# A two-layer hybrid block with PEER experts: the PEER stage unrolled, v gathered by token and summed in column tiles, with rings of four buffers

## The chip, the cores and the metric

One core of one Trainium2 chip runs the whole program. The metric is the device time of one execution in microseconds. PE is TensorE, DVE VectorE, ACT ScalarE, POOL GpSimd, SP SyncE.

## What is computed

Two layers over 512 latent and 256 context tokens of width 1024, in float32. Each layer is a mixer (convolution, retention, mLSTM, windowed attention, a gated merge, an output projection) and then PEER, a feed-forward part made of experts, on which the change falls. Layer 0 applies PEER to all 768 tokens (6 blocks of 128), layer 1 to the 512 latent tokens (4 blocks).

```python
def block(xb):                                   # 128 tokens
    q = (xb @ wq).reshape(-1, HEADS, 2, half)
    s = jnp.einsum('nhcd,ckd->nhck', q, keys)    # 8 heads, 2 sides, 128 keys
    sv, si = lax.top_k(s, 16)
    cand = sv[:, :, 0, :, None] + sv[:, :, 1, None, :]
    cv, ci = lax.top_k(cand.reshape(..., 256), 16)
    expert = i1 * 128 + i2                       # i1, i2 picked from si by ci
    gate = jax.nn.softmax(cv, axis=-1)
    u_sel, v_sel = u[expert], v[expert]          # (n, 8, 16, 1024) each
    act = gelu(einsum('nd,nhkd->nhk', xb, u_sel))
    return einsum('nhk,nhkd->nd', gate * act, v_sel)
```

Each token thus needs 128 rows of `u` and 128 rows of `v`, its 128 slots (head h, rank k, n = 16 h + k), and each row is 4 KB. A block gathers 2 x 128 x 128 rows.

## The kernel before

All engines run through stages in the same order; at a stage's start each waits for all to have ended the one before. The stages of a layer are norm, ret, mlstm, attn, merge, out, peerq, route, peer. Every result of PE outside the PEER sum goes through a rotation of PSUM banks: `bank(name)` takes the next one and first waits until the bank taken `BANKS` names earlier has been read (`BANKS` is 8).

The stage peer is a loop (`eng.Fori`) on each engine over the blocks of `peer_calls(l)`: one loop over the 2 context blocks and one over the 4 latent blocks in layer 0, one over 4 in layer 1. In a block:

- POOL issues one indirect DMA per slot. `u` of slot n brings to partition p the row of token p (L2000), into a ring of 8 buffers of 128 x 1024. `v` of slot n does the same (L2008) into another ring of 8, and follows 16 slots behind `u`: 16 `u` alone, then 112 times `u` and `v` in turn, then 16 `v` alone. `u` waits for the dot that frees its buffer, `v` for the PE sum that frees its own. POOL issues in program order, so what waits holds up all behind it.
- DVE takes the dot product of each landed `u` with the block's activations (L1566). Between the dots it does the routing of the next block in pieces (`route_part`): `top_keys` and `candidates` in heads 0 to 3, one of them after every fourth dot; `pick_keys` twice in head 4 (it ends at L1481); small ones after. It does so in the last block of a layer too, whose result nobody reads. After each head `weigh` multiplies gates and activations.
- ACT takes the gelu of a head's 16 dots and then makes 16 diagonal 128 x 128 matrices of weights (L1891), in a ring of 8.
- PE multiplies each diagonal with its `v` (L854, L856) and accumulates all 128 slots in banks 6 and 7: tokens are rows there.
- At the block's end DVE waits for the last sum, scales it in PSUM (L1577), and adds it to the residual (L1581, L1586). The next block begins with copies (L1526 to L1533) and its first dot.

## Time and profile before

| what | value |
|---|---|
| median of 3 runs | 7287.52 us (7281.2 to 7294.59) |
| the profiled execution | 7279.13 us, its span 7277.3 us |
| PE, DVE, ACT, POOL busy | 5493.0, 3590.4, 967.0, 2810.0 us |
| moved | 1580.75 MB, of it 1363.67 MB by POOL's queue |
| gathers | 1280 of `u`, 1280 of `v` |

The span runs from the first to the last instruction; some microseconds of an execution lie around it. Busy time is a mean over stages with different limits, so the stage is read by itself: POOL is busy only in PEER, from 2055 to about 4309 us and from 5758 to about 7260 us, and there the DMA engines are busy nearly all the time.

### The profile page before, as it was taken

What the parts mean: (1) busy time and instruction counts of PE and PEld (TensorE: products, weight loads), DVE (VectorE), ACT (ScalarE), POOL (GpSimd) and SP (SyncE); (2) the same over time, 40 slices, a digit from 0 to 9 for tenths busy, and PEclk for the clock granted to TensorE, in tenths of its full rate; (3) what the DMA queues carried; (4) which work ended last, traced back from release to release, by engine and by line L of the source; (5) the groups of instructions that cost most, each with busy time, mean ns of one, the idle gap of its engine ahead of it and who ended that gap; (6) DMA issues with size and microseconds to landing.
All of it is one profiled execution on the core that took longest, in us unless ns stands there. A gap on an engine that the chain in (4) does not pass through costs nothing. (4 is left out here: it accounts for less than half of the span.)

```text
span 7277.3 us, 56488 instructions
## 1 busy us (share of the span) xinstructions
PE 5493.0 (75%) x16472; PEld 2983.1 (41%) x16472; DVE 3590.4 (49%) x7999; ACT 967.0 (13%) x2360; POOL 2810.0 (39%) x2627
## 2 busy tenths in 40 slices
PE   3869699999966666656666668788999765766666
PEld 1545657556632222222222235465646422222222
DVE  1565645112455555656565635455312664646474
ACT  1102012000011111111111120111200111111111
POOL 0000000000057677767676740000000276767676
PEclk7979785999988888889888889888699888888888
DMA  8101100111279999999999971021023599999998
GB/s 331 41 12 41 64 24 1 67 52 64 93 256 375 337 368 353 371 343 370 348 369 335 370 277 47 29 73 32 13 92 103 183 368 344 369 353 372 341 363 343
DMA packets 556363, 1580.75 MB, mean 217 GB/s; under 512 B 73665, under 2 KB 207297, under 8 KB 555953
## 3 DMA queue, kind: packets, MB, share of 16 engines
q0 software_dynamic: 374032, 1363.67, 49.7%
q1 hardware_dynamic: 182048, 213.91, 8.9%
q8 instruction: 105, 1.72, 0.1%
q14 instruction: 178, 1.45, 0.1%
HBM read 1572.95 MB, written 4.44 MB: 217 GB/s over the span
## 5 line engine op out<-in xcount | busy, mean ns | idle before, releaser
L854 PE MATMUL bank<-arena 128*128 128x512 f32 x2560 | 1443.7, 647 | 1292.0 <-ACT arena L1891 1028.8
L2000 POOL DMA_INDIRECT arena<-in_peer_u,arena x1280 | 1354.0, 1058 | 2509.4 <-issue 2383.1
L1566 DVE CUSTOM_DVE_ANT_0 arena<-arena 128x1024 f32<-128x1024 f32 x1280 | 1551.3, 1225 | 1174.8 <-DMA arena<-in_peer_u,arena 1149.3
L2008 POOL DMA_INDIRECT arena<-in_peer_v,arena x1280 | 1421.6, 1111 | 420.5 <-issue 294.8
L856 PE MATMUL bank<-arena 128*128 128x512 f32 x2560 | 1371.3, 619 | 0.0
L854 PEld LDWEIGHTS bank<-arena 128*128 128x128 f32 x2560 | 482.0, 203 | 2090.6 <-ACT arena L1891 1095.9
L516 PE MATMUL bank<-arena 128*128 128x512 f32 (+3 forms) x2880 | 935.3, 488 | 4.8 <-DVE arena L949 3.2
L856 PEld LDWEIGHTS bank<-arena 128*128 128x128 f32 x2560 | 513.5, 201 | 665.4 <-issue 665.4
L516 PEld LDWEIGHTS bank<-arena 128*128 128x128 f32 x2880 | 533.5, 193 | 400.2 <-issue 338.7
L1891 ACT ACTIVATE arena<-arena 128x128 f32<-128x128 f32 x1280 | 453.3, 395 | 1600.4 <-PE bank L856 894.1
L781 PE MATMUL bank<-arena 128*128 128x512 f32 (+1 forms) x1536 | 569.2, 524 | 1.7 <-ACT arena L1805 1.7
L781 PEld LDWEIGHTS bank<-arena 128*128 128x128 f32 x1536 | 294.2, 192 | 260.5 <-issue 244.6
L1927 POOL DMA_DIRECT2D arena<-in_mlstm_gate_b x8 | 4.1, 522 | 811.4 <-DVE arena L1080 811.4
L1356 DVE TENSOR_TENSOR arena<-bank,arena 128x256 f32<-128x256 f32 (+1 forms) x72 | 43.4, 603 | 535.2 <-PE bank L786 535.2
L786 PE MATMUL bank<-arena 128*128 128x512 f32 (+1 forms) x768 | 290.7, 522 | 0.0
L1882 ACT ACTIVATE arena<-arena 128x16 f32<-128x16 f32 x80 | 17.4, 217 | 1616.2 <-DVE arena L1566 1616.2
L527 PE MATMUL bank<-arena 128*128 128x256 f32 (+1 forms) x960 | 193.9, 365 | 28.6 <-DVE arena L895 28.6
L989 DVE SCALAR_TENSOR_TENSOR arena<-arena 128x512 f32<-128x512 f32 (+1 forms) x360 | 207.0, 658 | 0.0
L786 PEld LDWEIGHTS bank<-arena 128*128 128x128 f32 x768 | 146.2, 190 | 128.7 <-issue 122.3
L527 PEld LDWEIGHTS bank<-arena 128*128 128x128 f32 x960 | 171.7, 195 | 53.4 <-issue 32.7
L1927 POOL DMA_DIRECT2D arena<-mlstm_rows x24 | 12.8, 536 | 403.8 <-DVE arena L1249 133.9
L1577 DVE TENSOR_TENSOR bank<-bank,arena 128x512 f32<-128x512 f32 x20 | 13.0, 694 | 292.5 <-PE bank L856 292.5
(270 smaller groups left out, 4628.0 us busy)
## 6 DMA issues: line engine op xcount, KB each, us to landing
arena<-in_w_in SPq DMA_DIRECT2D x74, 1024.0 KB, 5.3
arena<-in_mod_w SPq DMA_DIRECT2D x24, 2048.0 KB, 18.1
arena<-in_peer_wq SPq DMA_DIRECT2D x32, 1024.0 KB, 5.6
arena<-in_peer_u,arena POOLq DMA_INDIRECT x1280, 6.2
arena<-in_peer_v,arena POOLq DMA_INDIRECT x1280, 6.3
arena<-mlstm_rows POOLq DMA_DIRECT2D x24, 768.0 KB, 4.4
arena<-in_w_branch SPq DMA_DIRECT2D x32, 512.0 KB, 6.3
arena<-mod_rows SPq DMA_DIRECT2D x16, 512.0 KB, 8.0
```

The source lines that it names most:

```text
L516: i = mm(b[:, 0:n], w[:, k, m * P:(m + 1) * P], HTk[:, k, t0:t0 + n], start=(k == 0), stop=(k == KD - 1))
L527: i = mm(b[:, 0:n], HTk[:, k, t * P:(t + 1) * P], w[:, k, c0:c0 + n], start=(k == 0), stop=(k == KD - 1))
L781: i = mm(b[:, 0:n], wg[:, k, m * P:(m + 1) * P], HTk[:, k, t0:t0 + n], start=(k == 0), stop=(k == KD - 1))
L786: i = mm(b[:, 0:n], wb[:, k, m * P:(m + 1) * P], YSb[:, i_ * BB + k, t0:t0 + n], start=(k == 0), stop=(k == BB - 1))
L854: mm(banks[6][:, :], G["diag"][:, n % DRING, :], G["v"][n % VRING][:, 0:512], start=(n == 0), stop=(n == SLOTS - 1))
L856: mm(banks[7][:, :], G["diag"][:, n % DRING, :], G["v"][n % VRING][:, 512:1024], start=(n == 0), stop=(n == SLOTS - 1)).then_inc(fl.sem("v ...
L989: v.scalar_tensor_tensor(dst, src, tap, dst, ALU.mult, ALU.add).then_inc(*dv.step())
L1356: v.tensor_tensor(PRD[:, 0:n], b[:, 0:n], g, ALU.mult).then_inc(*dv.step("read", ("branch", l, j, i_, m, t0)))
L1566: v.tensor_tensor_reduce(u, u, G["hb"], 1.0, 0.0, ALU.mult, ALU.add, G["dots"][:, n:n + 1])\
L1891: act(G["diag"][:, n % DRING, :], ident, ACT.Copy, scale=G["w"][:, n:n + 1])\
L2000: eng.indirect_dma_start(G["u"][n % URING], None, utab, bass.IndirectOffsetOnAxis(G["idxu"][:, n:n + 1], 0))\
L2008: eng.indirect_dma_start(G["v"][n % VRING], None, vtab, bass.IndirectOffsetOnAxis(G["idxv"][:, n:n + 1], 0))\
```

## The change

- The loops go: each engine's program is written out for all blocks, waits are for constants, and the copies at a block's start go (buffers alternate by block instead). `route_part` is left out in a layer's last block.
- `v` is gathered by token: gather n brings to partition p the row of slot p of token n. For this the indices are transposed on PE (`turned`, `turned_indices`), and so are the weights; ACT's `spread` writes them into two zeroed tensors so that `token_weights(G, n)` is a 128 x 32 matrix with one filled column. The diagonals go.
- PE sums token n with four matmuls of 128 x 32 by 128 x 256, one in each column tile (`tile_position=(0, 32 * j)`). A row of PSUM is then a token within its group of 32, and a tile holds 256 of its columns; after the scaling, SP turns the result back to tokens by columns with 16 small DMAs a block (`yp` to `yt`), and DVE adds it later.
- A layer with B blocks has B + 1 passes. In pass x POOL issues `u` of block x and `v` of block x - 1 in turn: the first pass is `u` alone, the last `v` alone.
- The rings of `u` and `v` have 4 buffers each, and the rotation of banks has 6, since banks 6 and 7 are kept for the sums.

```diff
-BANKS = 8
-URING, VRING, DRING = 8, 8, 8
+BANKS = 6
+URING, VRING = 4, 4
+IDX_RING = 3
...
+def peer_blocks(l):
+    first = 0 if l == 0 else NB + (l - 1) * (NB - CB)
+    return [(first + x, t) for x, t in enumerate(out_blocks(l))]
...
+            ws = [HT[:, 2 * D:2 * D + 64 * 32], ws1]
+                        idxu=[iu.bitcast(U32)[:, x * SLOTS:(x + 1) * SLOTS] for x in range(2)],
+                        idxt=[it.bitcast(U32)[:, x * SLOTS:(x + 1) * SLOTS] for x in range(IDX_RING)],
+                        gate=[gt[:, x * SLOTS:(x + 1) * SLOTS] for x in range(2)],
+                        u=ring[:URING], v=ring[URING:URING + VRING],
...
+        def token_weights(G, n):
+            g, m = divmod(n, 32)
+            return G["ws"][g // 2][:, g % 2, 32 * m:32 * m + 32]
...
-                for b0, nb, base in peer_calls(l):
-                    with eng.Fori(0, nb) as i:
-                        for n in range(SLOTS):
-                            if n == 0:
-                                eng.wait_ge(fl.sem("residual_added"), i + base + 1)
-                            eng.wait_ge(fl.sem(f"v_landed{n % VRING}"), (i + base) * (16 * SLOTS // VRING) + 16 * (n // VRING + 1))
-                            eng.wait_ge(fl.sem("diagonal_ready"), (i + base) * SLOTS + n + 1)
-                            mm(banks[6][:, :], G["diag"][:, n % DRING, :], G["v"][n % VRING][:, 0:512],
-                               start=(n == 0), stop=(n == SLOTS - 1))
-                            mm(banks[7][:, :], G["diag"][:, n % DRING, :], G["v"][n % VRING][:, 512:1024],
-                               start=(n == 0), stop=(n == SLOTS - 1)).then_inc(fl.sem("v_summed"), 1)
+                def turned(name, src, ready):
+                    b = bank(name)
+                    eng.wait_ge(*at(*ready))
+                    nc.tensor.transpose(b[:, 0:P], src, ident).then_inc(*pe.step("full", name))
+                def v_sum(it, n):
+                    g, m = divmod(n, 32)
+                    if n == 0:
+                        eng.wait_ge(*at("spread", it))
+                        if it > peer_blocks(l)[0][0]:
+                            eng.wait_ge(*at("y_scaled", it - 1))
+                    eng.wait_ge(*at("v_landed", it, n))
+                    for j in range(COLS):
+                        i = mm(banks[6 + g // 2][32 * j:32 * j + 32, (g % 2) * W:(g % 2 + 1) * W], token_weights(G, n),
+                               G["v"][(it * SLOTS + n) % VRING][:, j * W:(j + 1) * W], start=(m == 0), stop=(m == 31),
+                               tile_position=(0, 32 * j))
+                    i.then_inc(*pe.step("v_summed", it, n))
+                blocks = [it for it, _ in peer_blocks(l)]
+                turned(("idxT", blocks[0]), G["i2"], ("experts", blocks[0]))
+                for it in blocks + [blocks[-1] + 1]:
+                    for n in range(SLOTS):
+                        if it > blocks[0]:
+                            v_sum(it - 1, n)
+                        if n == (HEADS - 1) * TOPK and it + 1 in blocks:
+                            turned(("idxT", it + 1), G["i2"], ("experts", it + 1))
+                    if it in blocks:
+                        turned(("wT", it), G["w"], ("weighed", it, HEADS - 1))
...
+                def turned_indices(r, it):
+                    eng.wait_ge(*at("full", ("idxT", it)))
+                    v.tensor_copy(G["idxt"][it % IDX_RING], bank_of(("idxT", it))[:, 0:P]).then_inc(*r.step("idxt", it))
+                    fl.mark(("read", ("idxT", it)), r.sem)
...
+                for a in G["ws"]:
+                    v.memset(a, 0.0).then_inc(*dv.step("spread_zero", l))
+                turned_indices(dv, first)
...
+                def scaled_sum(it, t):
+                    s = 0 if t >= CB else 1
+                    if it > first:
+                        eng.wait_ge(*at("y_turned", it - 1))
+                    eng.wait_ge(*at("v_summed", it, SLOTS - 1))
+                    for half in range(2):
+                        v.tensor_tensor(G["yp"][:, half * 512:half * 512 + 512].rearrange("p (g c) -> p g c", g=2),
+                                        banks[6 + half][:, :].rearrange("p (g c) -> p g c", g=2),
+                                        G["ga"][:, s * W:(s + 1) * W].unsqueeze(1).to_broadcast([P, 2, W]), ALU.mult)\
+                            .then_inc(*dv.step("y_scaled", it))
+                def added_sum(it, t):
+                    eng.wait_ge(*at("y_turned", it))
+                    v.tensor_tensor(Xb[:, t, :], Xb[:, t, :], G["yt"], ALU.add).then_inc(*dv.step("x_done", it))
...
+                blocks = peer_blocks(l)
+                for x, (it, t) in enumerate(blocks):
+                    for h in range(HEADS):
+                        for k in range(TOPK):
+                            n = h * TOPK + k
+                            u = G["u"][(it * SLOTS + n) % URING]
+                            eng.wait_ge(*at("u_landed", it, n))
+                            v.tensor_tensor_reduce(u, u, G["H2"][:, t * D:(t + 1) * D], 1.0, 0.0, ALU.mult, ALU.add,
+                                                   G["dots"][:, n:n + 1]).then_inc(*dv.step("dot", it, n))
+                            if h and k == 3:
+                                weigh(it, h - 1)
+                            if it + 1 <= blocks[-1][0]:
+                                route_part(it + 1, STORE[:, x * NSCORE:(x + 1) * NSCORE], h, k)
+                            if x and h == 1 and k == 0 and x > 1:
+                                added_sum(it - 2, t - 2)
+                    weigh(it, HEADS - 1)
+                    if x:
+                        scaled_sum(it - 1, t - 1)
+                scaled_sum(it, t)
+                added_sum(it - 1, t - 1)
+                added_sum(it, t)
...
+                def spread(it):
+                    eng.wait_ge(*at("spread_zero", l))
+                    if it > peer_blocks(l)[0][0]:
+                        eng.wait_ge(*at("v_summed", it - 1, SLOTS - 1))
+                    eng.wait_ge(*at("full", ("wT", it)))
+                    b = bank_of(("wT", it))
+                    for half in range(2):
+                        act(G["ws"][half][:, :, 0:1024:33], b[:, half * 64:half * 64 + 64].rearrange("p (g m) -> p g m", g=2),
+                            ACT.Copy).then_inc(*sc.step("spread", it))
+                    fl.mark(("read", ("wT", it)), sc.sem)
+                for it, _ in peer_blocks(l):
+                    for h in range(HEADS):
+                        gelu(it, h)
+                        if h == HEADS - 3 and it + 1 <= peer_blocks(l)[-1][0]:
+                            gate_exp(it + 1)
+                    spread(it)
...
+                def u_gather(it, n):
+                    x = it * SLOTS + n
+                    if n == 0:
+                        eng.wait_ge(*at("idxu", it))
                         eng.sem_inc(fl.sem("gathers_allowed"), 1)
-                        for h in range(HEADS + 1):
-                            if h == 1:
-                                eng.wait_ge(fl.sem("v_indices_staged"), it + 1)
-                                eng.wait_ge(fl.sem("v_summed"), it * SLOTS + 1)
-                                eng.sem_inc(fl.sem("gathers_allowed"), 1)
-                            for k in range(TOPK):
-                                n = h * TOPK + k
-                                if h < HEADS:
-                                    if n >= URING:
-                                        eng.wait_ge(fl.sem("dots_done"), it * SLOTS + n - URING + 2)
-                                        eng.sem_inc(fl.sem("gathers_allowed"), 1)
-                                    eng.indirect_dma_start(G["u"][n % URING], None, utab,
-                                                           bass.IndirectOffsetOnAxis(G["idxu"][:, n:n + 1], 0))\
-                                        .then_inc(fl.sem(f"u_landed{n % URING}"), 16)
-                                if h:
-                                    n -= TOPK
-                                    if n >= VRING:
-                                        eng.wait_ge(fl.sem("v_summed"), it * SLOTS + n - VRING + 2)
-                                        eng.sem_inc(fl.sem("gathers_allowed"), 1)
-                                    eng.indirect_dma_start(G["v"][n % VRING], None, vtab,
-                                                           bass.IndirectOffsetOnAxis(G["idxv"][:, n:n + 1], 0))\
-                                        .then_inc(fl.sem(f"v_landed{n % VRING}"), 16)
+                    if x - URING >= peer_blocks(l)[0][0] * SLOTS:
+                        eng.wait_ge(*at("dot", *divmod(x - URING, SLOTS)))
+                        eng.sem_inc(fl.sem("gathers_allowed"), 1)
+                    fl.done(eng.indirect_dma_start(G["u"][x % URING], None, utab,
+                                                   bass.IndirectOffsetOnAxis(G["idxu"][it % 2][:, n:n + 1], 0)),
+                            f"u_landed{x % URING}", ("u_landed", it, n), by=16)
+                def v_gather(it, n):
+                    x = it * SLOTS + n
+                    if n == 0:
+                        eng.wait_ge(*at("idxt", it))
+                        eng.sem_inc(fl.sem("gathers_allowed"), 1)
+                    if x - VRING >= peer_blocks(l)[0][0] * SLOTS:
+                        eng.wait_ge(*at("v_summed", *divmod(x - VRING, SLOTS)))
+                        eng.sem_inc(fl.sem("gathers_allowed"), 1)
+                    fl.done(eng.indirect_dma_start(G["v"][x % VRING], None, vtab,
+                                                   bass.IndirectOffsetOnAxis(G["idxt"][it % IDX_RING][:, n:n + 1], 0)),
+                            f"v_landed{x % VRING}", ("v_landed", it, n), by=16)
+                blocks = [it for it, _ in peer_blocks(l)]
+                for it in blocks + [blocks[-1] + 1]:
+                    for n in range(SLOTS):
+                        if it in blocks:
+                            u_gather(it, n)
+                        if it > blocks[0]:
+                            v_gather(it - 1, n)
...
-                        dma(G["ga"][:, s * D:(s + 1) * D], modr[l, s:s + 1, 5 * D:6 * D].to_broadcast([P, D]), "ga2_loaded")
+                        for j in range(COLS):
+                            dma(G["ga"][32 * j:32 * j + 32, s * W:(s + 1) * W],
+                                modr[l, s:s + 1, 5 * D + j * W:5 * D + (j + 1) * W].to_broadcast([32, W]), "ga2_loaded")
                     fl.mark(("ga2", l), "ga2_loaded")
                     if l + 1 < DEPTH:
                         layer_vectors(l + 1)
+                    for it, t in peer_blocks(l):
+                        eng.wait_ge(*at("y_scaled", it))
+                        if it > peer_blocks(l)[0][0]:
+                            eng.wait_ge(*at("x_done", it - 1))
+                        for g in range(4):
+                            for j in range(COLS):
+                                dma(G["yt"][32 * g:32 * g + 32, j * W:(j + 1) * W],
+                                    G["yp"][32 * j:32 * j + 32, g * W:(g + 1) * W], "y_turned")
+                        fl.mark(("y_turned", it), "y_turned")
```

What stands on POOL at the start of layer 0's stage, before (the first two gathers wait for `dots_done` of the block before and then of the ring; the register instructions work out what to wait for):

```order
L2000 DMA arena<-in_peer_u,arena 128x1024 [waits dots_done]
L2000 DMA arena<-in_peer_u,arena 128x1024 x7
L1998 REGISTER_ALU
L2000 DMA arena<-in_peer_u,arena 128x1024 [waits dots_done]
L1998 REGISTER_ALU
L2000 DMA arena<-in_peer_u,arena 128x1024 [waits dots_done]
L1998 REGISTER_ALU
L2000 DMA arena<-in_peer_u,arena 128x1024 [waits dots_done]
```

After, from the ring's second round in the first pass to the first `v` (`peer0_vector` counts DVE's steps of the stage, the dots among them):

```order
L1993 DMA arena<-in_peer_u,arena 128x1024 x3
L1993 DMA arena<-in_peer_u,arena 128x1024 [waits peer0_vector] x125
L2006 DMA arena<-in_peer_v,arena 128x1024 [waits peer0_vector]
L1993 DMA arena<-in_peer_u,arena 128x1024 [waits peer0_vector]
L2006 DMA arena<-in_peer_v,arena 128x1024
L1993 DMA arena<-in_peer_u,arena 128x1024 [waits peer0_vector]
L2006 DMA arena<-in_peer_v,arena 128x1024
```

The first pass holds 128 `u` and no `v` (three and 125 of them stand here, after the first one), and what bounds its pace is a wait for the dot four slots back; before, `v` joined after 16 `u` and the wait was for the dot eight back.

What stands on DVE from the last dots of a block to the next, before (ISA is the dot and the reading of its sum):

```order
L1566 ISA arena<-arena 128x1024 [waits u_landed7]
L1566 ISA arena 128x1
L1572 COPY arena<-arena 128x128
L1541 REGISTER_ALU
L1542 TENSOR_TENSOR arena<-arena 128x16 [waits gelu_done]
L1575 ISA
L1577 TENSOR_TENSOR bank<-bank,arena 128x512 [waits v_summed]
L1577 TENSOR_TENSOR bank<-bank,arena 128x512
L1581 ISA [waits y_scaled]
L1581 TENSOR_TENSOR arena<-arena,bank 128x512
L1586 ISA [waits half_added,indices_staged]
L1586 TENSOR_TENSOR arena<-arena,bank 128x512
```

After, from the last dot of layer 0's second block on:

```order
L1580 ISA arena<-arena 128x1024 [waits u_landed3]
L1580 ISA arena 128x1
L1536 TENSOR_TENSOR arena<-arena 128x16 [waits peer0_scalar]
L1562 TENSOR_TENSOR arena<-bank,arena 128x512 [waits peer0_tensor]
L1562 TENSOR_TENSOR arena<-bank,arena 128x512
L1580 ISA arena<-arena 128x1024 [waits u_landed0]
L1580 ISA arena 128x1
L1580 ISA arena<-arena 128x1024 [waits u_landed1]
L1580 ISA arena 128x1
L1580 ISA arena<-arena 128x1024 [waits u_landed2]
L1580 ISA arena 128x1
```

The wait for `v_summed` stood for this block's own last `v`, with nothing of the next block ahead of it; now the wait (`peer0_tensor`) is for the block before, whose last `v` is gathered next to this block's last `u`, and the dots of the next block follow directly.

## Rows read from the trace of the kernel before

**Rows 1.** The page's first line.

```profile
span 7277.3 us, 56488 instructions
```

**Rows 2.** Windows (busy us and count per engine, PEclk, DMA share, GB/s).

```profile
2055.00:4310.00 2255.00, 1478.79 (x3072) 598.02 (x3072) 1310.44 (x3025) 301.72 (x836) 1668.55 (x1536) 0.86 0.95 358
...
2455.66:2767.25 311.59, 210.24 (x432) 84.10 (x432) 193.25 (x444) 44.08 (x122) 243.88 (x223) 0.87 0.98 370
...
2686.02:2767.25 81.23, 58.93 (x123) 23.84 (x121) 38.92 (x66) 14.65 (x37) 62.32 (x63) 0.89 1.01 394
```

**Rows 3.** Timeline, POOL: first gathers of four stretches (start, duration).

```profile
2055.47 1.38 POOL L2000 DMA_INDIRECT arena<-in_peer_u,arena  x1 [1156.04 <-issue]
...
2419.93 0.94 POOL L2000 DMA_INDIRECT arena<-in_peer_u,arena  x1 [3.57 <-issue]
...
2793.04 0.93 POOL L2000 DMA_INDIRECT arena<-in_peer_u,arena  x1 [0.30 <-issue]
...
5758.57 1.42 POOL L2000 DMA_INDIRECT arena<-in_peer_u,arena  x1 [824.56 <-issue]
```

**Rows 4.** Timeline, DVE, from one block to the next.

```profile
2396.73 1.23 DVE L1566 CUSTOM_DVE_ANT_0 arena<-arena 128x1024 f32<-128x1024 f32 x1 [1.30 <-DMA arena<-in_peer_u,arena]
...
2428.39 1.30 DVE L1577 TENSOR_TENSOR bank<-bank,arena 128x512 f32<-128x512 f32 x2 [29.96 <-PE bank L856]
...
2438.27 1.22 DVE L1566 CUSTOM_DVE_ANT_0 arena<-arena 128x1024 f32<-128x1024 f32 x1 [0.28 <-DVE arena L1533]
```

**Rows 5.** Timeline, DVE, the end of both layers' PEER.

```profile
4306.07 1.30 DVE L1577 TENSOR_TENSOR bank<-bank,arena 128x512 f32<-128x512 f32 x2 [29.17 <-PE bank L856]
...
4308.43 0.69 DVE L1586 TENSOR_TENSOR arena<-arena,bank 128x512 f32 x1 [0.22 <-DVE arena L1581]
...
7259.27 0.69 DVE L1586 TENSOR_TENSOR arena<-arena,bank 128x512 f32 x1 [0.22 <-DVE arena L1581]
```

**Rows 6.** Timeline, POOL, a gather in the middle of a block.

```profile
2386.40 0.93 POOL L2008 DMA_INDIRECT arena<-in_peer_v,arena  x1 [0.30 <-issue]
```

**Rows 7.** Source lines L2000, L2008, three stretches: issue to landing.

```profile
L2000 POOL DMA_INDIRECT arena<-in_peer_u,arena x1: 936/936/936, 2419.9 to 2419.9; - x1
...
DMA to landing us min/median/max: 4.4/4.4/4.4
...
L2008 POOL DMA_INDIRECT arena<-in_peer_v,arena x5: 936/937/939, 7237.1 to 7244.0; - x5
...
DMA to landing us min/median/max: 5.1/5.2/5.6
...
L2000 POOL DMA_INDIRECT arena<-in_peer_u,arena x94: 933/937/2434, 2499.3 to 2759.6; - x94
...
DMA to landing us min/median/max: 5.3/6.2/6.6
```

**Rows 8.** Window, eight dots with routing; timeline, DVE, `pick_keys` and dots.

```profile
2078.26:2093.52 15.26, 0.00 (x0) 0.00 (x0) 14.27 (x42) 0.22 (x1) 11.23 (x10) 0.50 0.89 309
...
2610.61 0.22 DVE L1468 TENSOR_SCALAR arena<-arena 128x128 uint32<-128x128 uint32 x1
...
2618.59 1.25 DVE L1566 CUSTOM_DVE_ANT_0 arena<-arena 128x1024 f32<-128x1024 f32 x1
...
2619.77 1.21 DVE L1566 CUSTOM_DVE_ANT_0 arena<-arena 128x1024 f32<-128x1024 f32 x1
```

**Rows 9.** Timeline, PE: column tiles (L560), a v product (L856).

```profile
101.11 1.91 PE L560 MATMUL bank<-arena 128*2 128x256 f32 x32 [1.65 <-DMA arena<-in_mod_w]
...
2403.30 1.02 PE L856 MATMUL bank<-arena 128*128 128x512 f32 x2
```

**Rows 10.** Timeline, PE, layer 1's retention, `rv_tok`.

```profile
4503.47 22.72 PE L527 MATMUL bank<-arena 128*128 128x256 f32 x91 [18.28 <-DVE arena L895]
```

**Rows 11.** Timeline, SP's small loads; the page's DMA issues.

```profile
5745.63 0.81 SPq L2018 DMA_DIRECT2D arena<-mod_rows  x2
...
arena<-in_w_in SPq DMA_DIRECT2D x2, 64.0 KB, 2.4
```

196 lines of the change are left out of this document (58 added, 138 removed).

## The prediction

> **What bounds the kernel now.** I read the page's first lines for the span [rows 1], then the windows of PEER [rows 2], then one block on the timelines of POOL and DVE. Outside PEER the change touches only the rotation of banks, so the question is PEER. In layer 0's stage the DMA engines have a busy share of 0.95 while PE works 1479 of 2255 us and DVE 1310: neither can be the bound. The second row of [rows 2] is the stretch of one block from `u` 16 to `u` 127, 111 pairs of gathers in 311.6 us: 2.81 us a pair, 1.40 a gather, DMA share 0.98. The third is its last 31 pairs, `u` 96 to `u` 127, in which DVE does no routing but for small ends: 81.2 us, 2.62 a pair. POOL by itself needs 0.93 us and a gap of 0.30 for a gather [rows 6], 1.23 us, so it is never far behind the DMA engines. A block is therefore bound by the transfer of its 256 gathers, and beside that by its edges: the first gathers of blocks 1 and 2 are 373.1 us apart [rows 3], though 128 x 2.81 are only 359.3. At the edge DVE ends its last dot at 2398, waits 30 us for the sum of the last sixteen `v`, and starts the next dot at 2438.3, 40.3 us later [rows 4]; meanwhile PE runs the `v` that POOL issues alone at four rows of 0.43 us a slot, 1.72 us (the second of [rows 9]), and DMA share is lost. From the first gather to the last residual, layer 0 takes 4309.1 - 2055.5 = 2253.6 us and layer 1 takes 7260.0 - 5758.6 = 1501.4 us [rows 3, 5].
>
> **The middle passes.** Where `u` and `v` are issued in turn and the next block is routed (4 passes in layer 0, 2 in layer 1) I take the pair's 2.81 us for all 128 pairs: 359.3. The edge goes: `v` of block x - 1 is gathered beside `u` of block x, and its last sum comes within about 2 us of DVE's last dot, less than a buffer's slack. SP's turning moves 0.5 MB per block, the size of one gather: 1.4 us. The ring of 4 has to be checked. A `u` buffer is needed again after four pairs, 11.2 us; it is free after 6.2 us to landing (the third pair of [rows 7]), some 0.1 of signal, 1.23 of dot and 0.15 until POOL starts (my estimates, each below POOL's plain gap of 0.30): 7.7 us, a slack of 3.5. Dots without a wait follow every 1.18 us (2618.59, 2619.77 [rows 8]); eight of them with one `top_keys` and one `candidates` took 15.26 us, so such a piece is about 2.9 us. DVE's idle time of 1.6 us in each pair takes half of it and the slack the rest: nothing. `pick_keys` takes 8.0 us (2610.61 to 2618.59 [rows 8]): less 1.6 and 3.5 it stops POOL for 2.9 us, twice a pass. Landing is 6.2 us under load against 4.4 alone [rows 7], so 1.8 us of it is queue that still feeds the DMA engines; between 1.1 and 2.9 us are lost each time, 4 a pass. Sum 365 a pass. Bounds: 337 (the rate of the last 31 pairs in all of it) and 385 (below, the ring).
>
> In a layer's last middle pass nothing is routed now. That was hidden work, but the pairs without it are the faster ones: 128 x 2.62 + 1.4 = 337 us, once a layer.
>
> **The first pass, `u` alone.** The DMA engines and POOL could go at about 1.3 us a gather. In heads 0 to 3 DVE can't: 15.26 us for 8 slots [rows 8] is 1.91 each, 122 us for 64. In heads 4 to 7 the ring is the bound: landing, 0.1, 1.23, 0.15, for four slots. Landing is 4.4 us alone; with gathers 1.72 us apart it was 5.2 (the second pair of [rows 7]); 6.2 is the other bound. With 5.2 it is 6.7 us, 1.67 a slot, 107 us. Two `pick_keys` lengthen one turn of the ring each, to 4 x 1.18 + 8.0 = 12.7: 12 us. 6 us to the first dot, less 5 because the next pass's first gather needs only the fourth last dot: 242 us. The bounds 4.4 and 6.2 give 229 and 258.
>
> **The last pass, `v` alone.** The diagonals and their 1.72 us a slot go. For the column tiles the trace has a neighbour, the adaLN product: 32 rows, four groups of four tiles (each matmul is two rows), in 1.91 us, 0.48 a group [rows 9]; one after another they would be as long as 1.72. PE waits between tokens here and may be granted its lower level; at the block's start the window shows PE at mean clock 0.50 while idle [rows 8]. I take 0.75 us, between 0.5 and 1.0. A turn is 5.2 + 0.1 + 0.75 + 0.15 = 6.2 us, 1.55 a token, 198 us, and 2 at the start, when `spread` waits for the last weights: 200. The bounds of landing give 174 and 230.
>
> **The end of a layer.** From the last `v` issued: 5.2 landing, 0.9 PE, two scalings of 0.69, an addition of the block before (1.2, estimated from two of 0.69), then 16 DMAs of SP at about 0.4 us each (two small loads took 0.81 [rows 11]) and 2.4 to landing (the last row there), then the last addition, 1.2, and signals: 19 us. This wait is new; before, DVE went from PSUM to the residual at once.
>
> **Banks.** With 6 instead of 8 in rotation PE stops two banks sooner wherever it runs far ahead. The waits show one such place in each layer: in retention PE stops until DVE has read a rope bank (L895), 18.3 us in layer 1, and then goes on with `rv_tok` [rows 10]. A bank of `rv_tok` is 8 matmuls of 256 columns, each two rows of half of 0.43 us [rows 9]: 3.4 us. Two banks fewer are in hand when the stop ends, 6.9 us, and DVE waits for them next. Twice, 14 us; the lower bound is 0, if other waits take it up, the upper 30, if the shorter chains of mLSTM stop as well. Loop jumps, copies and the diagonals of ACT all lie beside transfers: nothing, but for what is in the edge.
>
> **The sum.** Layer 0: 242 + 4 x 365 + 337 + 200 + 19 = 2258, 4 more than before. Layer 1: 242 + 2 x 365 + 337 + 200 + 19 = 1528, 27 more: it has the same two lone passes for four blocks. With 14 for banks 45 us are added to the profiled execution's 7279.1: 7324. That execution is 8 us below the median of the runs, so I predict 7330 for the median. What is gained, some 8 to 9 us at each edge and 36 in a pass without routing, is given back by two passes a layer that a ring of 4 can't fill.
>
> **The rivals.** *The ring runs dry in the middle too.* Landing reached 6.6 us at most in [rows 7] but POOL's own row there reached 2.4; if both coincide with routing hardly any slack is left, and eight pieces cost 1.3 each and two `pick_keys` 6.4 each: 23 us a pass instead of 4, six times 19 more, 7444. For it: POOL issues in order, so a late `u` holds `v` too. Against it: the median landing is what counts mostly.
> *The other side: middle passes run at the rate of the pairs without routing.* What slows the routed pairs from 2.62 to 2.81 is then not routing but what goes with DVE's backlog after an edge and with PE's and ACT's traffic, all of which the change takes away. Six passes lose 28 us each: 7162. It decides from 7.5 us a pass on. Against it: PE and ACT do the same work in the last 31 pairs, which are fast.
> *A shorter landing.* If four in flight land as one does, in 4.4 us [rows 7], the first pass is 229 and the last 174: 7252.
> The Trainium skill, page "DMA: Bandwidth & Descriptors", section "Anatomy of one DMA — SWDGE (gpsimd) path", gives a gather about 2.0 us fixed plus its bytes over 436 GB/s, which for 512 KB is an estimate of 3.2 us; by this rule four buffers would keep the engines full, the lone passes would cost about 165 and 218 us, and the sum would be near 7210. The trace disagrees as it stands, with 4.4 us alone and 5.2 in sequence, though 0.94 of either is POOL's own row.
> *The tiles don't run side by side*: 1.24 us more in each turn of the last pass, 40 us a layer, 7410. The adaLN rows speak against it.
>
> **How the numbers follow.** The sum 0.42 (own range 7280 to 7385), the dry ring 0.20, serial tiles 0.05, the faster middle 0.21, the shorter landing 0.12. Half of the dry ring and half of the faster middle lie outside 7170 to 7450. The bound for a change is 0.2%, 15 us around 7287.5: faster has the faster middle, most of the shorter landing and 0.03 of the sum's tail, 0.34; within it 0.14; slower 0.52.
>
> **What the profile after would show.** Middle passes: first gathers 365 us apart, DMA share 0.97, no gap of DVE at the edge. The first pass: DVE's dots at 1.91 us in heads 0 to 3, then idle before `u`, with POOL released by the dot. The last: POOL idle before each `v`, 1.55 us apart, released by PE. After it a wait of DVE for SP, near 9 us. The place of `rv_tok`: PE idle 25 us instead of 18. Wrong makes it above all a middle pass that is 8 us shorter or 10 longer, and next a landing unlike 5.2 us.

## The result, and the profile after

The changed kernel takes **7487.64 us** (median of 4 runs, 7471.27 to 7509.63), the kernel before beside it on the same chip 7284.36 (4 runs): a ratio of **1.028, 95% interval 1.025 to 1.031**. It is slower, as forecast (slower had a chance of 0.52), but by 203 us where I had 45, and outside the range.

The page of the profile after, its head; beside [rows 1]:

```profile
span 7483.7 us, 59947 instructions
...
PE 4430.8 (59%) x21612; PEld 2249.2 (30%) x21612; DVE 3477.3 (46%) x7499; ACT 507.4 (7%) x1090; POOL 2776.5 (37%) x2627
...
PEclk7979785999955555555555558877799655555555
DMA  8101100211268999999999851120123579999997
```

The span is 206.4 us longer than that of [rows 1]. Every digit of DMA in the inner part of PEER is a 9, but on either side of it the digits fall off: a lone pass stands at each end.

The windows of layer 0's PEER after: the first pass, four middle passes with routing, the middle pass without, the last pass (columns as in [rows 2]):

```profile
2077.60:2352.90 275.30, 0.45 (x1) 0.18 (x1) 213.16 (x494) 5.68 (x11) 158.58 (x128) 0.51 0.75 242
2352.90:3805.90 1453.00, 553.56 (x4080) 104.15 (x4080) 870.18 (x1998) 20.06 (x52) 1111.83 (x1025) 0.50 0.98 371
3805.90:4147.20 341.30, 138.77 (x1025) 25.96 (x1025) 161.74 (x269) 2.13 (x10) 259.29 (x256) 0.50 1.02 395
4147.20:4387.40 240.20, 137.10 (x1025) 26.15 (x1025) 4.00 (x9) 0.78 (x3) 120.14 (x127) 0.51 0.85 284
```

The middle runs as the kernel before did in its inner part: share 0.98 and 1.02, 371 and 395 GB/s, against 0.98 and 1.01, 370 and 394 in [rows 2]. In the two lone passes the DMA engines have shares of 0.75 and 0.85, and no other engine is full: DVE works 213 of 275 us, PE 137 of 240, POOL 159 and 120. A stretch in which nothing is full must be bound by a chain of waits. Timeline of the first pass in head 7, DVE:

```profile
2313.45 1.23 DVE L1580 CUSTOM_DVE_ANT_0 arena<-arena 128x1024 f32<-128x1024 f32 x1 [1.16 <-DMA arena<-in_peer_u,arena]
...
2315.77 1.23 DVE L1580 CUSTOM_DVE_ANT_0 arena<-arena 128x1024 f32<-128x1024 f32 x1 [1.09 <-DMA arena<-in_peer_u,arena]
...
2320.63 1.22 DVE L1580 CUSTOM_DVE_ANT_0 arena<-arena 128x1024 f32<-128x1024 f32 x1 [0.76 <-DMA arena<-in_peer_u,arena]
```

and POOL in the same stretch:

```profile
2315.49 0.94 POOL L1993 DMA_INDIRECT arena<-in_peer_u,arena  x1 [1.15 <-DVE arena L1580]
2317.81 1.29 POOL L1993 DMA_INDIRECT arena<-in_peer_u,arena  x1 [1.39 <-DVE arena L1580]
```

DVE waits for a landing, POOL for a dot: the ring of four. The dot at 2313.45 ends at 2314.68 and POOL starts the gather that it frees at 2315.49, 0.81 us later; the next, 2317.00 to 2317.81, likewise. The gather of 2315.49 is read by the dot at 2320.63, 5.14 us on. The same in the last pass, PE and POOL:

```profile
4199.00 0.94 POOL L2006 DMA_INDIRECT arena<-in_peer_v,arena  x1 [0.37 <-issue]
...
4199.82 1.08 PE L847 MATMUL bank<-arena 128*32 128x256 f32 x8 [1.66 <-DMA arena<-in_peer_v,arena]
...
4201.74 0.94 POOL L2006 DMA_INDIRECT arena<-in_peer_v,arena  x1 [1.80 <-PE bank L847]
...
4204.30 1.08 PE L847 MATMUL bank<-arena 128*32 128x256 f32 x8 [0.26 <-DMA arena<-in_peer_v,arena]
```

A token's four column tiles (eight rows) take 1.08 us. The group at 4199.82 ends at 4200.90, POOL starts at 4201.74: 0.84 us. Over the gathers of a lone pass of layer 0 the medians are: from the issue of `u` to its dot 5.8 us (5.5 in heads 5 to 7), from the dot's end to the freed issue 1.12 (least 0.81); from the issue of `v` to PE 5.46, from PE's end to the freed issue 0.84 (least and median). In the `u` pass a few turns are much longer, so that the means are 6.18 and 1.23: with the dot's 1.23 they make 8.6 us, 2.16 a slot, and 128 of these are the pass's 275 us.

The median of 1.12 hides two levels. Of 124 freed `u` gathers 37 start 0.81 or 0.82 us behind the dot, and in all of them the dot ended 1.26 us or more after POOL's previous issue; 69 start 1.0 to 1.25 us behind it, mostly 1.12, and there the dot ended sooner after that issue (0.47 us in the median). A gather of POOL and its gap take 0.94 + 0.30 = 1.24 us.

The end of layer 0, timeline, which answers to [rows 5]:

```profile
4387.45 0.94 POOL L2006 DMA_INDIRECT arena<-in_peer_v,arena  x1 [0.33 <-issue]
...
4394.05 1.29 DVE L1562 TENSOR_TENSOR arena<-bank,arena 128x512 f32<-128x512 f32 x2 [239.04 <-PE bank L847]
4395.25 1.22 DVE L1570 TENSOR_TENSOR arena<-arena 128x1024 f32<-128x1024 f32 x1
4396.54 10.00 SPq L2024 DMA_DIRECT2D arena<-arena  x16
4407.83 1.23 DVE L1570 TENSOR_TENSOR arena<-arena 128x1024 f32<-128x1024 f32 x1 [11.36 <-DMA arena<-arena]
```

The layer ends 21.6 us after its last `v` issue. The 206.4 us of the span come out of starts and ends like these: 22.1 before layer 0's first gather (2077.60, against the first of [rows 3]), 77.9 in its PEER (2331.5 us, first gather to last residual, against 2253.6), 7.5 between the layers, 99.2 in layer 1's PEER (from 5866.1 to 7466.7, 1600.6 us, against 1501.4), and nothing behind.

### The profile page after: what moved, and what is told of

Same layout as the page of the kernel before. It is cut to its first block and busy times, and to the rows that moved or that the text cites. A ratio compares the mean times of both kernels' runs of the same rounds, so it can differ in the third digit from the quotient of the medians.

```text
span 7483.7 us, 59947 instructions
## 1 busy us (share of the span) xinstructions
PE 4430.8 (59%) x21612; PEld 2249.2 (30%) x21612; DVE 3477.3 (46%) x7499; ACT 507.4 (7%) x1090; POOL 2776.5 (37%) x2627
## 3 DMA queue, kind: packets, MB, share of 16 engines
q14 instruction: 125, 1.02, 0.0%
## 5 line engine op out<-in xcount | busy, mean ns | idle before, releaser
L847 PE MATMUL bank<-arena 128*32 128x256 f32 x10240 | 1382.0, 633 | 1952.9 <-DMA arena<-in_peer_v,arena 1945.8
L1993 POOL DMA_INDIRECT arena<-in_peer_u,arena x1280 | 1385.7, 1083 | 2561.7 <-issue 2304.2
L2006 POOL DMA_INDIRECT arena<-in_peer_v,arena x1280 | 1356.1, 1059 | 568.3 <-issue 347.9
L847 PEld LDWEIGHTS bank<-arena 128*32 128x32 f32 x10240 | 258.5, 140 | 3067.1 <-DMA arena<-in_peer_v,arena 3048.7
L502 PEld LDWEIGHTS bank<-arena 128*128 128x128 f32 x2880 | 533.7, 193 | 405.7 <-issue 337.0
L767 PEld LDWEIGHTS bank<-arena 128*128 128x128 f32 x1536 | 294.1, 192 | 261.4 <-issue 245.1
L513 PE MATMUL bank<-arena 128*128 128x256 f32 (+1 forms) x960 | 193.0, 364 | 42.7 <-DVE arena L899 42.7
L513 PEld LDWEIGHTS bank<-arena 128*128 128x128 f32 x960 | 170.8, 194 | 67.7 <-DVE arena L899 43.5
L772 PEld LDWEIGHTS bank<-arena 128*128 128x128 f32 x768 | 145.9, 190 | 129.1 <-issue 122.4
L836 PEld LDWEIGHTS bank<-arena 128*128 128x128 f32 x20 | 3.6, 179 | 575.3 <-issue 568.4
L725 PEld LDWEIGHTS bank<-arena 128*128 128x128 f32 x640 | 146.1, 334 | 0.0
```

Source lines behind the costliest of these rows:

```text
L502: i = mm(b[:, 0:n], w[:, k, m * P:(m + 1) * P], HTk[:, k, t0:t0 + n], start=(k == 0), stop=(k == KD - 1))
L513: i = mm(b[:, 0:n], HTk[:, k, t * P:(t + 1) * P], w[:, k, c0:c0 + n], start=(k == 0), stop=(k == KD - 1))
L725: i = mm(b[:, 0:AD], A["PT"][:, h % 2, x * P:(x + 1) * P], A["V"][:, j, g * AD:(g + 1) * AD], start=(x == 0), stop=(x == len(kb) - 1))
L767: i = mm(b[:, 0:n], wg[:, k, m * P:(m + 1) * P], HTk[:, k, t0:t0 + n], start=(k == 0), stop=(k == KD - 1))
L772: i = mm(b[:, 0:n], wb[:, k, m * P:(m + 1) * P], YSb[:, i_ * BB + k, t0:t0 + n], start=(k == 0), stop=(k == BB - 1))
L847: i = mm(banks[6 + g // 2][32 * j:32 * j + 32, (g % 2) * W:(g % 2 + 1) * W], token_weights(G, n), G["v"][(it * SLOTS + n) % VRING][:, j * ...
```

## Experiments

The theory is that **the ring's turn** sets the lone passes: 5.5 + 1.22 + 1.12 = 7.84 us over four `u`, 1.96 a slot where no routing stands between the dots, and 5.45 + 1.08 + 0.84 = 7.37 over four `v`, 1.85 a token (1.87 in the trace). The rival is that lone gathers transfer more slowly in themselves. All experiments ran on chips other than the first, in groups, each beside the kernel before, which took 7447 us (the first four kernels), 7445 (the next three), 7419 (the next four) and 7446 (the last four). Times are given as ratios to it, and passes are compared within those chips. The changed kernel itself stands on the third and fourth of these chips. On the first, the kernel with routing put back (below) has the same lone passes, four buffers each, and serves as their reference: 273 and 272 us, and 241 and 243.

The changed kernel there, as the reference:

> The changed kernel itself, beside the kernel before on the chip that ran the last seven kernels. There the kernel before took 7446 us, 2.2% over its first time, with its gathers in pairs moving some 355 GB/s in place of 370. If the change's ratio of 1.028 holds, 7655 us; the ring's turns (1.96 and 1.85 us) don't depend on the transfer rate, so the lone passes stay at 275 and 241 us and the middle ones grow to about 380 us: 14 us by 8 passes over the first profile, about 7600 us (7560 to 7660). The first experiments are read against this one.

7652.43 us, 1.0323 (1.0308 to 1.0339); the chip was another than the one that the text expected. And once more, on the chip of the last four:

> The changed kernel, as the reference of the three that follow on one chip: 1.028 to 1.033 of before.

7682.01 us, 1.0319 (1.0305 to 1.0333). The ratio is a little above the first one. The middle passes with routing took 378 to 388 us instead of 360 to 367, the lone ones 270 to 272 and 240 to 244 instead of 275 and 243 to 245 (the last pass counted from the last `u` issue, here and below): the transfer-bound passes grew, the lone passes did not. That speaks for the ring already.

**Seven buffers each.**

```diff
-URING, VRING = 4, 4
+URING, VRING = 7, 7
```

> The changed kernel with seven u and seven v buffers in place of four and four, nothing else. Theory A (the turn of a four-buffer ring sets the lone passes: issue to dot 5.5 us + 1.22 dot + 1.12 to the next issue = 7.84 us over 4 buffers = 1.96 a slot; v 7.37/4 = 1.85 a token): with seven the turns are 1.12 and 1.05, under what else limits a slot, so the u pass of each layer falls from 275 and 285 us to about 222 and the v pass from 240 to about 170, the middle passes hardly move: about 250 us less than the changed kernel, 7240 us (7180 to 7290). Rival B (the transfers themselves are slower in the lone passes, from the addresses by token or the clock, whatever the number of buffers): the lone passes keep more than 80% of their time and the whole stays above 7430 us.

7469.7 us, 1.0033 (1.0021 to 1.0045). (The 285 us of layer 1 in the expectation is a slip: that pass took 275.4.) The last pass of layer 0 with four buffers on this chip, from the kernel with routing put back, window:

```profile
4275.00:4514.90 239.90, 137.06 (x1017) 25.81 (x1017) 4.20 (x9) 0.79 (x3) 119.90 (x128) 0.51 0.86 285
```

and with seven the two lone passes of layer 0:

```profile
2076.50:2304.20 227.70, 0.45 (x1) 0.18 (x1) 209.32 (x493) 5.68 (x11) 156.05 (x128) 0.51 0.86 291
...
4184.60:4381.10 196.50, 136.78 (x1013) 26.14 (x1012) 5.16 (x9) 0.78 (x3) 121.74 (x130) 0.52 0.96 346
```

The last pass went from a share of 0.86 to 0.96 and from 241 us to 197, with the same groups of 1.08 us on PE, the same granted clock (0.51 and 0.52) and the same addresses; the first went from 273 to 228, and in its heads 1 to 3 the slots now follow at 1.92 us, DVE's pace, predicted as 1.91. By the bounds that I had set neither side wins: the total lies far outside theory A's 7180 to 7290, and above the rival's 7430, and the lone passes kept 82 to 87% of their time, the rival's "more than 80%". Those bounds were set badly: the total was written for the first chip, and the 80% leaves no room for DVE's pace and for the transfers, which take over once the ring doesn't bind. What decides is the number of buffers: the rival says that it changes nothing, and with nothing else changed all four lone passes fell, by 37 to 46 us each. The ring is shown as what bound them. Nor is much left for slower lone gathers: with seven buffers they moved 346 GB/s in the last pass, and pairs 353 to 361 in windows of the middle passes. The forecast of 7240 us was made from the first chip's transfers; in the ratio, 0.994 expected and 1.003 found, most of the gap is in the last passes, which stopped at 1.50 to 1.53 us a token instead of 1.3. A pair in the middle took 2.93 on this chip, 1.47 a gather, and the share there and in the last pass is 0.96: that is the transfers' own pace on this chip.

**Eight `u`, four `v`** (the edit is `URING, VRING = 8, 4`).

> The changed kernel with eight u buffers and still four v buffers. Theory A: only the first pass of each layer gets shorter (275 to about 222, 285 to about 222), the last pass stays at 240 us: about 115 us less, 7370 us. Rival B: nothing beyond 20 us. Should the v pass move too, the rings do not act separately.

7589.27 us, 1.0193 (1.0175 to 1.021). The first passes took 230 and 228 us, the last 241 and 241. Each ring has its own pass, and each gives somewhat over a per cent: `u` 1.3 (97 us, of the 115 expected), `v` the other 1.6.

**Five buffers each** (`URING, VRING = 5, 5`).

> The changed kernel with five u and five v buffers. Theory A: the turn of u, 7.84 us over 5 is 1.57, which lies under the vector engine's 1.92 in heads 0 to 3 and a little over what the transfers allow in heads 5 to 7; of v 7.37 over 5 is 1.47, at the 1.5 us that seven buffers reached. So the fifth buffer alone gives nearly all that seven gave: first passes about 235 us, last passes about 197 us, within 20 us of the kernel with seven. A rival that the gain grows with every buffer puts five about a third of the way.

7508.27 us, 1.0125 (1.0108 to 1.0143). First passes 246 us, last passes 208: two thirds of what seven gave, not nearly all. The miss is in the landing: with five in flight the median from the issue of `v` to PE was 5.9 us in layer 0 and 6.0 in layer 1, not 5.45, so the turn was (5.9 + 1.92)/5 = 1.56 where 1.47 was expected; the tokens followed at 1.58 and 1.60 in the mean. With more gathers in flight each took longer to land, so a longer ring lengthened its own turn.

**Banks**, on the kernel before:

```diff
-BANKS = 8
+BANKS = 6
```

> The kernel before with six matmul banks in its rotation in place of eight, nothing else. The changed kernel reached its first gather 22 us later in layer 0 and lost some 9 us in layer 1. If that is the banks, this kernel is about 28 to 30 us slower than before (7312 us). If it is where the longer program code or something else of the change lies, it is within 5 us of before.

7473.4 us, 1.0037 (1.0025 to 1.0049), 26 us. Its first gather came at 2077.8 us, where the changed kernel has 2077.6. The 22 us ahead of layer 0's PEER are the banks.

**Routing put back into the last block**, its result used by nobody:

```diff
+                            else:
+                                if h < HEADS // 2 and k in (3, 11):
+                                    top_keys(dv, STORE[:, (x - 1) * NSCORE:x * NSCORE], 2 * h + k // 8)
+                                if h < HEADS // 2 and k in (7, 15):
+                                    candidates(dv, 2 * h + k // 8)
+                                if h == HEADS // 2 and k in (4, 12):
+                                    pick_keys(dv, k // 8)
```

> The changed kernel with the key search of another block (top_keys, candidates, pick_keys; its results are used by nobody) added on the vector engine in each layer's last block, where the changed kernel has none. The middle passes that carry a search took 359 to 365 us, the one without 341. Theory: the search costs its work beyond what the transfers hide, so this pass goes to about 363 us and the whole up by about 45 us (two layers), 7530 us. Rival: 341 is set by the 256 transfers of the pass alone at the best rate and search work is hidden up to it, and the longer passes come from something else (indices, gates and transposes between blocks): then no change.

7707.19 us, 1.0352 (1.0337 to 1.0368), against 1.032 without. The last block took 382.5 us in layer 0 and 381.9 in layer 1, where the changed kernel took 370 to 375 on two other chips, and kernels with longer rings 372 to 378 on this one. The sign is right, the size is 4 to 12 us and not the 22 that I had read from the first chip, and the difference of the ratios is close to its interval. That slower transfers cover more of the search would explain it but was not tested, and neither were the 22 us on the first chip.

**Four buffers each in the kernel before** (`URING, VRING, DRING = 4, 4, 8`).

> The kernel before with four u and four v buffers in place of eight and eight (eight diagonals as before). A slot there has one u and one v gather, and took 2.60 us at best by the transfers; four slots are 10.4 us, more than a turn (u about 7.8, v about 7.4 plus the wait for the weight of its slot). Theory A: the rings of four cost little where u and v alternate, 20 to 120 us over the whole kernel, most of it at the edges of blocks. Rival: the alternating pitch itself is set by the turn, and the kernel is slower than the changed one (above 7490 us).

8083.48 us, 1.0858 (1.0842 to 1.0875): far off what I expected. Timeline at a head's boundary, POOL:

```profile
2373.68 0.94 POOL L2000 DMA_INDIRECT arena<-in_peer_u,arena  x1 [0.30 <-issue]
2383.44 0.94 POOL L2008 DMA_INDIRECT arena<-in_peer_v,arena  x1 [8.82 <-PE bank L856]
```

and what PE waits for, on ACT:

```profile
2378.40 2.45 ACT L1891 ACTIVATE arena<-arena 128x128 f32<-128x128 f32 x8 [10.95 <-DVE arena L1542]
```

The fifth `v` of a head needs a buffer whose sum needs the head's weights, and those are formed four dots into the next head. Eight buffers reach across that, four don't, and POOL stops once in each head. To see whose ring it is, four `u` and eight `v` (`URING, VRING, DRING = 4, 8, 8`):

> The kernel before with four u buffers and still eight v buffers. With four of both it took 8083 us, 636 us over before, where 20 to 120 were expected; its trace shows one wait of 8 to 9 us in each head, of the v gather for TensorE (whose sum of the fifth v back needs the weights of its head, ready only after the first four dots of the next head). If that is the cause, it belongs to the v ring, and this kernel stays within 120 us of before (7450 to 7570). If u's ring has a part of it, this one is above 7700 us.

7511.22 us, 1.0125 (1.0109 to 1.014). So of 8.6% the shorter `v` ring adds 7.3. By gathering `v` a block later, the changed kernel has no such boundary; I take this as the reason why four buffers cost it 2.9% (from 1.032 to 1.003 with seven) and the kernel before 8.6%. The other 1.25%, 92 us, show the changed kernel's fault on a small scale: each block of the kernel before begins with 16 `u` alone. From the first `u` to the first `v` a block takes 43 to 46 us with four `u` buffers (34.6 in a layer's first block) and 36 to 38 (26) with eight, the same on two chips. Over ten blocks that is 72 of the 92 us.

**No counting instruction.** Ahead of each gather, behind its wait, POOL increments a semaphore that nobody waits for. Taken out in all its four places (one is shown), with the wait kept:

```diff
-                        eng.sem_inc(fl.sem("gathers_allowed"), 1)
```

> The changed kernel without the counting instruction that follows the wait for a free buffer ahead of each gather. The blocked gather's issue started 0.81 us at the least and 1.12 in the median after the dot that freed its buffer. If that instruction and its queue are part of this, the turn falls by up to 0.3 us (0.07 a slot; 20 to 30 us over the four lone passes together), 7460 us; if the delay is the wait's own and the preparation of the gather's issue, no change beyond 10 us.

7608.98 us, 1.0222 (1.0206 to 1.0237). Its trace had the least time from dot to issue at 0.28 us instead of 0.81, nearly twice the 0.3 that I had allowed for; but no changed kernel had run on its chip, so it was run again:

> The changed kernel without the counting instruction, now on the same chip as the changed kernel. Counting as part of the turn alone: the four lone passes shorten by 5 to 13 us each, 35 to 45 us in all, the middle passes not at all. Counting as a cost of every blocked gather: the middle passes shorten too, and the whole by 60 us or more.

7610.84 us, 1.0221 (1.0207 to 1.0235), 71 us under the changed kernel on the same chip. Timeline of its last pass, PE and POOL:

```profile
4303.09 1.08 PE L847 MATMUL bank<-arena 128*32 128x256 f32 x8 [0.18 <-DMA arena<-in_peer_v,arena]
...
4304.47 0.94 POOL L2002 DMA_INDIRECT arena<-in_peer_v,arena  x1 [0.33 <-PE bank L847]
```

From 4304.17 to 4304.47 are 0.30 us: 0.54 of the 0.84 went with the edit. That isn't the duration of the instruction. The source lines of the `v` wait show it, in the changed kernel and then in this one (duration in ns, least, median, most):

```profile
L2005 POOLq EVENT_SEMAPHORE  x1272: 17/17/17, 2361.3 to 7444.1; - x182
...
L2001 POOLq EVENT_SEMAPHORE  x8: 17/17/17, 2721.4 to 7352.1; - x8
```

With the count, wait and count are one instruction of 0.017 us of its own ahead of the gather; without it, the wait stands in the gather itself. So what cost 0.54 us is to have a separate semaphore instruction ahead of a blocked gather; whether the count or the separate wait does it, and where the time goes, no run tells.

The last passes fell by 13.5 and 14.8 us, as 0.54 x 128 / 4 = 17 would have it, less a landing up to 0.1 longer. The first fell only by 2.4 and 3.2. There the early level went from 0.81 to 0.28 us, but the late one stayed at 1.11 or 1.12, for 50 of 124 gathers in layer 0: it comes where the dot ends within 1.25 us of POOL's previous issue, with the instruction or without it. In the mean the issue came 0.30 us sooner behind the dot, and the landing and use took 0.2 longer. The middle passes fell by 3.5 us in the mean, which the turn doesn't explain.

**Seven buffers and eight banks.** In PEER the names that use a bank turn over six, elsewhere over eight (the edit's main lines):

```diff
-BANKS = 6
-URING, VRING = 4, 4
+BANKS = 8
+URING, VRING = 7, 7
...
-                    b = bank(name)
+                    j = len(peer_order)
+                    peer_order.append(name)
+                    banks_of[name] = j % 6
+                    if j >= 6:
+                        eng.wait_ge(*at("read", peer_order[j - 6]))
+                    b = banks[j % 6]
```

> The changed kernel with seven u and seven v buffers, and eight banks in the rotation again outside PEER (in PEER the names that use a bank turn over six, since banks 6 and 7 hold the sum of v). If the two costs add, it is 28 to 30 us under the kernel with seven buffers alone: about 7210 us, and faster than the kernel before by 1% (70 us).

7444.72 us, 1.000 (0.9991 to 1.001), and on the last chip

> Seven and seven buffers with eight banks, counting kept: 1.000 of before, as on the other chip.

7444.39 us, 0.9999 (0.999 to 1.0008). It isn't 1% faster than before, as I had expected from the first chip's transfers, but the two costs add up to all of the loss: 238 us below the changed kernel there, of which the lone passes have 168, the way to the two first gathers 30 and the middle passes 37. So a ring of four costs a little in the middle too, 4.7 us a pass here. The change as such, with its buffers and banks given back, is worth nothing either way on these two chips; on the first it was not run. And without the counting instruction:

> Seven and seven buffers, eight banks, and no counting instruction ahead of a gather. In the four-buffer kernel without that instruction the shortest time from a dot's end to the gather that it frees fell from 0.81 to 0.28 us, and from 0.84 to 0.30 behind TensorE. With seven buffers no turn sets a pass, so this should change nothing: 7440 us, 1.000 of before (0.997 to 1.003). If it is faster by more than 20 us, the counting costs something besides the turn.

7371.67 us, 0.994 (0.9927 to 0.9954), and beside its twin

> The same without counting: 0.994 of before again, 45 us less than with counting on the same chip, most of it in the middle passes (379 to 373 us each), if counting costs something besides the turn. If the difference was one between chips, the two agree within 10 us.

7395.27 us, **0.9931 (0.9917 to 0.9945)**: 49 us less than with counting, and faster than both kernels. My expectation of no change was wrong. Windows in middle passes, with counting:

```profile
2750.00:2950.00 200.00, 86.14 (x539) 18.05 (x536) 124.92 (x295) 0.87 (x4) 151.74 (x136) 0.53 0.97 355
3260.00:3460.00 200.00, 79.28 (x542) 16.02 (x538) 104.43 (x193) 4.14 (x9) 147.97 (x137) 0.52 0.97 359
```

and without:

```profile
2750.00:2950.00 200.00, 80.24 (x546) 15.49 (x540) 125.87 (x295) 0.87 (x4) 152.83 (x138) 0.50 0.97 362
3260.00:3460.00 200.00, 86.54 (x554) 18.60 (x554) 101.81 (x193) 4.14 (x9) 148.43 (x138) 0.51 0.98 364
```

The passes are 2 to 9 us shorter, all twelve parts of the two PEER stages have the same sign, and the rate is some 6 GB/s higher. That the gap in front of a gather costs a little even where POOL seems ahead is what this says; how it reaches the DMA engines stays open. The kernel before has the same instruction; it was not tried without it, since its waits are on a loop's register. So the 0.7% compares a kernel without the instruction with one that has it, and is not a gain of the change.

## Why the prediction was right or wrong

**The direction and its reason** were right: two lone passes in each layer that a ring of four can't fill. The direction was hardly more than even, 0.52; what made it clear is the cost that I had put too low. The eight middle passes were right one by one on this chip: with routing 365 forecast and 359.6 to 367.0 measured, without routing 337 forecast and 341 and 335 measured. On the other chips they took 370 to 388: the 2.81 us of a pair belong to the chip. The edge stall of [rows 4] did go, SP's turning is hidden, and neither the dry ring in the middle nor the faster middle passes took place. The end of a layer was forecast at 19 us and took 21.6 and 21.8: SP's sixteen DMAs needed 10.0 us in place of 6.4.

**The step that failed** is the ring's turn in the lone passes. Of the 161 us between my sum and the profile 148 are there: first passes 275 instead of 242 twice, last passes 240 and 241 instead of 200. The mechanism was the right one, the term was mis-sized. "0.15 until POOL starts" was an estimate for a wait that no row of the trace showed on its own; I took POOL's gap of 0.30 between unblocked gathers [rows 6] as its upper bound, which it is not. Measured, it is 0.84 us behind PE, and 0.81 at the least and 1.12 in the median behind a dot. Of the 0.84, 0.54 comes with a semaphore instruction that stands in the code between the wait and the gather, in both kernels, and that I had not priced; between unblocked gathers, as in [rows 6], it doesn't show. The 1.12 behind a dot is there with and without it, and its cause is open. PE's group was 1.08 us in place of 0.75: the granted clock is 0.50 to 0.51 in all four windows of layer 0's PEER above, the level of 1.2 GHz, where the kernel before had means of 0.86 to 0.89 [rows 2]. At that level a group's second four matmuls start 0.42 us after its first four and end 0.66 us later. The 0.48 of [rows 9] was a quarter of four groups that follow each other without a wait, at the upper level; a group by itself also has the end of its last matmul. The 0.75 was the middle of two levels, and the engine was at one of them. Landing was 5.45 to 5.5 with its signal, 5.3 in my sum. In all 7.84 instead of 6.7 and 7.37 instead of 6.2 us. In heads 0 to 3, too, the ring was the bound, at 2.12 us a slot, and not DVE's 1.91: this is 14 of the 33 us of the first pass, and 17 are heads 5 to 7, with 2.02 for 1.67.

The upper bounds that I had given for these passes, 258 and 230, varied landing alone, so that no end of them held the truth.

The rival of serial tiles falls: of the eight matmuls of a token four start within 0.02 us, and all end within 1.08 us at half the clock. So does the shorter landing, with 5.46 us in place of 4.4. The Trainium skill, page "DMA: Bandwidth & Descriptors", section "Anatomy of one DMA — SWDGE (gpsimd) path", by whose fixed cost and rate the last pass would by estimate have been some 165 us, gives the time of one transfer and none from the freeing of a buffer to the issue; the trace disagrees, with 240 us for four buffers and 197 for seven on another chip.

**Banks** were forecast at 14 us with 30 as a bound and cost 29.6 (22.1 + 7.5), in the experiment 26. The place that I had priced behaved as said; the profile page's group of that line, against [rows 10]'s:

```profile
L513 PE MATMUL bank<-arena 128*128 128x256 f32 (+1 forms) x960 | 193.0, 364 | 42.7 <-DVE arena L899 42.7
```

Both layers' waits there sum to 42.7 us, 28.6 before, and layer 1's is 25.6, as forecast (25). That is 14.1 us, the whole of the 14 that I had priced. The other 15 are in places that I had put only into the bound, layer 0 above all; which they are was not looked into.

## What to carry to other kernels

Where nothing is full, look for a ring: its pitch is (issue to landing + use + freeing to the next issue) over its buffers, and the last of the three needs a row of a *blocked* transfer. Look at every instruction between a wait and the DMA that it guards: here one of 0.017 us came with a delay of 0.54. A pipeline that puts producer and consumer side by side leaves each alone for one pass at either end, and there a ring sized for the pair has half the traffic to hide nearly the same latency; the fewer the blocks, the more those two passes weigh (99 us for four blocks, 78 for six).

## What the runs showed of the hardware

- The issue of a blocked gather started 0.28 to 0.30 us behind the event that freed its buffer where the gather itself waits, and 0.81 to 0.84 us behind it with a semaphore instruction of 0.017 us (wait and count) ahead of the gather. In the `u` passes it was 1.11 to 1.12 us in both cases where the dot ended soon after POOL's previous issue (within 1.25 us).
- From the issue of `v` to PE, 5.3 to 5.5 us with four gathers in flight, 5.9 to 6.0 with five, 6.1 to 6.3 with seven.
- The granted clock of TensorE was 0.50 to 0.51, its level of 1.2 GHz, in every pass of the changed kernel's PEER in layer 0: in the first, where it was idle, and in the others, where it worked in groups of eight matmuls of 32 columns of weights with waits between them. The kernel before, with full tiles, had 0.86 in the mean. No run here varies what PE does in a pass by itself, so what decides stays open.
- Five chips gave the kernel before 7284, 7445, 7447, 7419 and 7446 us. In windows of its middle passes the changed kernel moved 355 to 374 GB/s on the first and 341 to 352 on two others, while its lone passes took no longer there: 270 to 272 us for 275, and 240 to 244 for 243 to 245.
